# Hybrid decoder step in float32: tokens brought in already turned, and once more by rows

## What is computed

```python
h = rms_norm(x, norm1)                       # mean of squares over 2048 columns
z = h @ w_in                                 # 2048 -> 5120: u (1024), q, f, i, g (1024 each)
pool_out = pool_mix(u, ...)                  # trailing windows 2/4/8/16, per-group 256x256 matrix, pool_scale
o = hgrn2_recurrence(silu(q), 1 - forget, i, log(forget), S0)   # 8 heads, 128x128 state
o = rms(o) * hg_norm * silu(g)
x = x + concat([pool_out, o]) @ w_o          # 2048 -> 2048
h2 = rms_norm(x, norm2)
x = x + (silu(h2 @ w_gate) * (h2 @ w_up)) @ w_down   # 5632 wide
y = rms_norm(x, norm_f)                      # and the new pool and recurrence states
```

## Time and profile before

| what | value |
|---|---|
| median of 3 runs | 1410.99 us (1410.99 to 1411.94) |
| the profiled execution | 1411.39 us |
| its span | 1409.6 us |
| PE matmul busy | 1392.2 us (99%) |
| DVE, ACT, POOL busy | 775.2 us (55%), 579.4 us (41%), 206.9 us (15%) |
| HBM read | 206.43 MB |
| queue of SP | 203.16 MB, 52.6% of 16 engines' span |
| TensorE clock | granted 0.997 of full over the span |

### The profile page before, as it was taken

How to read it: one execution, slowest core, us unless ns; L and a number is a source line. 1 busy time by engine, 2 the same in 40 slices (tenths; PEclk the granted TensorE clock), 3 DMA queues, 4 the chain that set the end, 5 groups by cost and what they waited for, 6 DMA issues and landing times.

```text
span 1409.6 us, 27953 instructions
## 1 busy us (share of the span) xinstructions
PE 1392.2 (99%) x10208; PEld 1377.6 (98%) x10208; DVE 775.2 (55%) x1198; ACT 579.4 (41%) x966; POOL 206.9 (15%) x321
## 2 busy tenths in 40 slices
PE   8999999999999999999999999999999999999996
PEld 7999999999999999999999999999999999999996
DVE  6768888888655544444444444444444444444443
ACT  6535656666433333333333333333333333333443
POOL 0365444445222000000000000000000000000131
PEclk9999999999999999999999999999999999999998
DMA  9556555555655555545655545565554565555453
GB/s 270 145 143 183 152 151 166 165 151 151 166 149 149 149 149 149 149 123 146 179 149 149 149 130 144 146 176 149 149 149 129 146 172 148 149 149 139 124 144 116
DMA packets 408636, 214.53 MB, mean 152 GB/s; under 512 B 4286, under 2 KB 406542, under 8 KB 408597
## 3 DMA queue, kind: packets, MB, share of 16 engines
q1 hardware_dynamic: 389863, 203.16, 52.6%
q10 hardware_dynamic: 18742, 10.95, 2.7%
HBM read 206.43 MB, written 7.89 MB: 152 GB/s over the span
## 4 chain that ended last, share of the span: by engine, by line
PE 98%; DMA 1%; DVE 1%; ACT 0%; issue 0%; DVEq 0%; ACTq 0%
PE bank L426 31%; PE bank L427 31%; PE bank L428 31%; DMA w_raw<-in_w_in 1%; PE bank L540 1%; PE bank L656 0%; PE bank L473 0%; PE bank L698 0%; PE bank L631 0%; PE bank L700 0%; PE bank L699 0%; PE bank L585 0%; PE bank L640 0%; PE bank L755 0%; DVE a_lo L1255 0%; PE bank L618 0%
## 5 line engine op out<-in xcount | busy, mean ns | idle before, releaser
L426 PE MATMUL bank<-a_hi,w_hi 128*128 128x320 f32 x2016 | 627.1, 311 | 0.2
L428 PE MATMUL bank<-a_hi,w_lo 128*128 128x320 f32 x2016 | 623.7, 309 | 0.0
L427 PE MATMUL bank<-a_lo,w_hi 128*128 128x320 f32 x2016 | 623.6, 309 | 0.0
L1185 DVE TENSOR_TENSOR w_lo<-w_raw,w_hi 128x1024 fp32r<-128x1024 f32 (+1 forms) x412 | 457.5, 1151 | 137.5 <-ACT w_hi L813 136.3
L813 ACT ACTIVATE w_hi<-w_raw 128x1024 fp32r<-128x1024 f32 (+1 forms) x412 | 383.4, 967 | 161.0 <-PE bank L428 141.4
L426 PEld LDWEIGHTS bank<-a_hi,w_hi 128*128 128x128 f32 x2016 | 378.7, 188 | 2.4 <-issue 1.6
L427 PEld LDWEIGHTS bank<-a_lo,w_hi 128*128 128x128 f32 x2016 | 378.7, 188 | 0.7
L428 PEld LDWEIGHTS bank<-a_hi,w_lo 128*128 128x128 f32 x2016 | 378.6, 188 | 0.0
L426 PE MATMUL bank<-h_hi,w_hi 128*128 128x320 f32 x704 | 219.0, 311 | 0.0
L428 PE MATMUL bank<-h_hi,w_lo 128*128 128x320 f32 x704 | 217.8, 309 | 0.0
L427 PE MATMUL bank<-h_lo,w_hi 128*128 128x320 f32 x704 | 217.7, 309 | 0.0
(11 more groups left out here) (262 smaller groups left out, 1185.9 us busy)
## 6 DMA issues: line engine op xcount, KB each, us to landing
w_raw<-in_w_gate SPq DMA_DIRECT2D x44, 1024.0 KB, 5.6
w_raw<-in_w_up SPq DMA_DIRECT2D x44, 1024.0 KB, 5.6
w_raw<-in_w_down SPq DMA_DIRECT2D x64, 704.0 KB, 4.8
w_raw<-in_w_in SPq DMA_DIRECT2D x38, 1024.0 KB, 5.8
w_raw<-in_w_o SPq DMA_DIRECT2D x16, 1024.0 KB, 6.0
s<-in_state_hgrn ACTq DMA_DIRECT2D x8, 512.0 KB, 4.3
out<-sn ACTq DMA_DIRECT2D x8, 512.0 KB, 5.4
w_raw<-in_w_in SPq DMA_DIRECT2D x3, 512.0 KB, 8.1
```

What stands on the lines that cost most here:

```text
L426: pe.matmul(out, whi[:, par_, cols], r_hi, start=(k == 0), stop=False)
L427: pe.matmul(out, whi[:, par_, cols], r_lo, start=False, stop=False)
L428: last = pe.matmul(out, wlo[:, par_, cols], r_hi, start=False, stop=(k == last_k))
L1185: dve.tensor_tensor(wlo[:, par_, cols], raw[:, par_, cols], whi[:, par_, cols].bitcast(F32), SUB)\
```

## The change

- The host also lays the inputs out in three new arrays: `x_turned` (partition, tile, token), `w_first_two` (the first 256 columns of `w_in`, by partition), and `params` (all parameter vectors turned).
- `load_x` writes `x_turned` straight into `x1`, one transfer for a chunk. The 48 transposes of tokens, the 16 copies to `x1`, the two transposes of parameters and their copies go. ACT and DVE split from `x1`.
- The tokens by rows are still needed for the squares. They are loaded a second time, in two halves of 1024 columns with three transfers each (`load_tokens`): the first half behind the cache, the second behind the weights of unit 3.
- All squares of ACT stand later, behind the splits of unit 2; the spreading of 1/rms goes from k == 6 to k == 12 of unit 3; the last `lo_piece` of unit 3 goes ahead of the sums.
- `keep_busy` runs 5 matmuls in a row instead of 2 and 1.
- The identity is loaded behind the first chunks.

The diff, cut to its core:

```diff
@@ load_x, load_tokens, first_weights
+        def load_x(eng, chunk):
+            k0, k1 = CHUNKS[chunk]
+            eng.dma_start(x1[:, k0:k1, :], x_turned[:, k0:k1, :]).then_inc(x_loaded[chunk], 16)
+
+        def load_tokens(eng, half):
+            cols = slice(half * HD, (half + 1) * HD)
+            for i in range(2):
+                eng.dma_start(xt[:, i, cols], x_prompt[0, i * P:(i + 1) * P, cols]).then_inc(xt_loaded[half][i], 16)
+            eng.dma_start(xt[0:NS, 2, cols], x_sample.rearrange("b t d -> (b t) d")[:, cols])\
+               .then_inc(xt_loaded[half][2], 16)
...
-                          win_v[:, k0:k1, 0:2 * P]).then_inc(w_first[chunk], 16)
+                          w_first_two[:, k0:k1, :]).then_inc(w_first[chunk], 16)
@@ tensor
-            keep_busy(2)
-            pe.wait_ge(ident_loaded, 16)
-            pe.wait_ge(norm1_loaded, 16)
-            pe.transpose(TK[:, 0:KD], prow[0:KD, :], ident[0:KD, 0:KD]).then_inc(par_t, 1)
-            keep_busy(1)
-            pe.wait_ge(fill_done, 3)
-            pe.wait_ge(x_pad, 1)
-            for k in range(2):
-                x_transposes(k)
+            keep_busy(5)
...
-                for ahead in ((2, 3) if k == 0 else (k + AHEAD,)):
-                    if ahead < KD:
-                        x_transposes(ahead)
...
-                if k == 6:
+                if k == 12:
                     rms_first()
@@ scalar
-                act.wait_ge(xt_t, k + 1)
-                bk = (SA, SB, SC, TV)[k % 4]
-                act.activation(a_hi[:, k, :], bk[:, 0:N], ACT.Copy, scale=pcol("norm1", k)).then_inc(ahi_ready, 1)
-                if k in X_ACT:
-                    act.activation(x1[:, k, :], bk[:, 0:N], ACT.Copy).then_inc(xres_act, 1)
+                for chunk in range(5):
+                    if k == CHUNKS[chunk][0]:
+                        act.wait_ge(x_loaded[chunk], 16)
+                act.activation(a_hi[:, k, :], x1[:, k, :], ACT.Copy, scale=pcol("norm1", k)).then_inc(ahi_ready, 1)
@@ vector
+            dve.wait_ge(ident_loaded, 16)
             diagonals(6, rms_diag)
-            lo_piece(3, 1, 1, HALF[1])
```

More of the change, by code:

```diff
@@ L200, in hybrid_kernel @@
         hi_ready, lo_ready, piece_used, unit_read = (sem(n) for n in ("hi_ready", "lo_ready", "piece_used", "unit_read"))
-        ident_loaded, masks_loaded, norm1_loaded, par_loaded, wp_loaded, cache_loaded, s0_loaded = (
-            sem(n) for n in ("ident_loaded", "masks_loaded", "norm1_loaded", "par_loaded", "wp_loaded",
+        ident_loaded, masks_loaded, par_loaded, wp_loaded, cache_loaded, s0_loaded = (
+            sem(n) for n in ("ident_loaded", "masks_loaded", "par_loaded", "wp_loaded",
                              "cache_loaded", "s0_loaded"))
-        x_loaded = [[sem(f"x_loaded{chunk}{i}") for i in range(3)] for chunk in range(5)]
+        x_loaded = [sem(f"x_loaded{chunk}") for chunk in range(5)]
+        xt_loaded = [[sem(f"xt_loaded{half}{i}") for i in range(3)] for half in range(2)]
         w_first = [sem(f"w_first{chunk}") for chunk in range(5)]
[L206 to L209, removed]
+        first_hi, first_lo, w2_loaded, w3_loaded = (
+            sem(n) for n in ("first_hi", "first_lo", "w2_loaded", "w3_loaded"))
+        fill_done, lb_max, lb_exp, lb_ready = (
+            sem(n) for n in ("fill_done", "lb_max", "lb_exp", "lb_ready"))
         dve_link, newton_step = sem("dve_link"), sem("newton_step")
@@ L357, in load @@
                              view[:, bass.ds(k0, nk), bass.ds(col, P)]).then_inc(raw_loaded[par_], 16)
+            for chunk in range(5):
+                first_weights(sp, chunk)
+                if chunk >= 2:
+                    load_x(sp, chunk)
             sp.dma_start(cst[:, C_ID:C_ID + P], consts[:, C_ID:C_ID + P]).then_inc(ident_loaded, 16)
[L362 to L371, removed]
             sp.wait_ge(first_lo, 3)
@@ L827, in square @@
                 rows, at = (P if i < 2 else NS), 2 * i + half
-                for chunk in ((0, 1, 2), (3, 4))[half]:
-                    act.wait_ge(x_loaded[chunk][i], 16)
+                act.wait_ge(xt_loaded[half][i], 16)
                 after(act, ss_ready, squares[0])
@@ L1212, in _ @@
             dve.memset(epst[:, :], EPS).then_inc(fill_done, 1)
[L1213 to L1214 removed]
+            for bk in (SA, SB, SC):
+                dve.memset(bk[:, 2 * P:4 * P], 0.0)
             dve.memset(stat[:, :], 0.5).then_inc(fill_done, 1)
[L1216 to L1218 removed]
+            dve.wait_ge(par_loaded, 16)
             def lower_bound_max():
[L1222 to L1224 removed]
                 lb0 = 3 * KD
@@ L1261, in _ @@
             lo_piece(2, 0, 0, HALF[0])
-            for k in X_DVE[-2:]:
-                residual(k)
             lower_bound_max()
@@ L1266, in _ @@
             lo_piece(3, 1, 0, HALF[0])
+            lo_piece(3, 1, 1, HALF[1])
             dve.wait_ge(ss_ready, 6)
@@ L1652, in _ @@
         def _(pool):
-            pool.memset(xt[NS:P, 2, :], 0.0).then_inc(x_pad, 1)
             pool.wait_ge(ss_ready, 6)
@@ L1772 @@
     arrays["in_consts"] = constant_table(np)
+    tokens = np.concatenate([inputs["x_prompt"].reshape(TP, D), inputs["x_sample"].reshape(NS, D)])
+    arrays["in_x_turned"] = np.ascontiguousarray(tokens.T.reshape(KD, P, N).transpose(1, 0, 2))
+    first_two = inputs["w_in"][0][:, 0:2 * P].reshape(KD, P, 2 * P)
+    arrays["in_w_first_two"] = np.ascontiguousarray(first_two.transpose(1, 0, 2))
+    arrays["in_params"] = np.ascontiguousarray(
+        np.concatenate([inputs[name].reshape(rows, P) for name, rows in PARAMS]).T)
     args = [nc.dram_tensor(n, a.shape, mybir.dt.from_np(a.dtype), kind="ExternalInput").ap() for n, a in arrays.items()]
```

85 lines of the change are left out of this document (19 added, 66 removed).

## The result

| | before | after |
|---|---|---|
| median | 1411.11 us (13 runs, 1410.53 to 1412.03) | 1414.47 us (13 runs, 1413.44 to 1416.23) |
| ratio | | 1.0025, 95% interval 1.0017 to 1.0034 |
| profiled execution, span | 1411.39 us, 1409.6 us | 1415.68 us, 1413.6 us |
| granted clock over the span | 0.997 | 0.994 |

The kernel became slower by 3.4 us, just over the 0.2% that can be told from no change. The prediction had put 0.55 on no difference and 0.33 on slower. The time lies in the range and 0.3 us from the price of rival B, but it is not the forecast: A's own bounds ended at 1413.8 us. All 13 executions after show a granted clock of 0.994 or 0.995.

The account below looks back on a forecast made before the run. PE's chain was taken as the bound, its start nearly transfer-bound: 7.4 us gained early is eaten by waits of 3.7 and 4.9 us. Unit 4 starts 1.0 us later: 1411.4 + 1.0 = 1412.4, put at 1412.3 us; range 1408.5 to 1416.5.

Parts of the forecast that it names:

- rival B: Wait before unit 4: TensorE falls to its lower clock, costing 2 to 3 us, 1414.8 us in all; chance 0.30.
- A: The forecast case: transfers eat the start's gain, full clock stays; 1412.3 us, by itself 1410 to 1413.8; chance 0.47.
- the clock holds: Part of the forecast case: TensorE keeps its full clock through the 4.9 us standstill before unit 4.
- mark: Unit 4's first matmul, 45.09 us before, forecast at 46.1; the program from there on was to stay unchanged.
- Units 0 and 1 from 8.0 us, done at 22.2: Start of PE: 14.2 us of matmuls from 8.0 us if chunks keep up, ending 7.4 us earlier than before.
- The rate of the start, 365 GB/s: First transfers: 4.83 MB of tokens, first weights, parameters and identity at 365 GB/s from 2.6 us, there by 15.8 us.
- rival C: DMA queue runs faster than assumed: unit 4 starts at 41 to 42 us, about 1407.7 us; chance 0.12.
- Unit 3 at 33.1, waiting 3.7 us: PE before unit 3: waits 3.7 us for unit 3's weights, landing at 30.3 us, and starts at 33.1 us.
- Spreading of 1/rms costs some tenths, covered by the next wait: Unit 3, tile 12: late squares ready at 39 us against 38.9 us, at most some tenths, covered by the following wait.
- Unit 4's weights at 43.7, first matmul at 46.1, a standstill of 4.9 us: Before unit 4: weights land at 43.7 us, splits and handovers take 2.4 us, PE idles 4.9 us.
- Edits costed at nothing: Fewer ACT and DVE copies, POOL's memset, later keep_busy and later identity were each taken to cost nothing.
- Rival D: Doubled tokens run at the cache's 178 GB/s, or everything at 281: unit 4 at 52 us, 1417 to 1418; chance 0.11.

Follow-up runs that it names:

- e2_unit4_first: The changed kernel with unit 4's weights issued ahead of the masks and wp: 1410.86 us, 0.9997 of the kernel before.
- e6_both_orders: The changed kernel with unit 4's weights ahead of masks and wp, and samples' tokens in one transfer to 128 partitions (squares over other columns): 1408.93 us.
- e4_samples_128: The changed kernel with the samples' tokens in one transfer to 128 partitions instead of two to 64 (squares over other columns): 1411.90 us.
- e3_half_tokens: The changed kernel without the second half of the doubled tokens, all squares taken from the first half: 1411.09 us, 0.9998 of the kernel before.
- e5_first_rows: The changed kernel with the first two weight columns read from w_in in 1 KB rows again: 1414.95 us, 1.0025 of the kernel before.
- g1_samples_filled: The changed kernel with samples' tokens in one transfer to 128 partitions and matmuls of ones filling PE's waits before units 3 and 4: 1410.80 us.
- f1_squares_turned: The changed kernel without any second token load, squares taken from the turned tokens and summed by 16 PE matmuls: 1406.85 us, 0.9969 of before.

## Why the prediction was right, and where it was not

**The likeliest case missed one step: "the clock holds".** A gave 1412.3 us from a mark at 46.1 us. Its first half came true: the transfers ate the whole gain of units 0 and 1. Its second half did not, and rival B decided, with its mechanism, its place and nearly its price (2 to 3 us said, 2.5 measured, 1414.8 against 1414.47). That the total agrees to 0.3 us is partly luck: the mark came 0.7 us later than A's, and the profiled execution, which shows that mark, is 1.2 us above the median. The range held only because it took in B. B had a chance of 0.30 because of 3 us after the end of the program in which the clock still reads full, against a forecast standstill of 4.9 us. B asked for a standstill that outlasts those 3 us, and that was too strict: a mean of 0.87 over the window from 44 to 46 us is half speed for its last 0.5 us, so the clock fell some 2.5 us after PE went idle at 43.04 us. The row of the end was also one sample of a scattered time. All ten traces end with the same work, and the clock falls between 0.5 us (`e2_unit4_first`) and 3.2 us (before) after the last matmul: 1.7 us in after, 3.0 us in `e6_both_orders`. The Trainium skill, TensorE: Matmul & The Clock Gate, "HAM oscillation — how this bites in real kernels", describes waits for DMA from which each tile comes back cold; the 0.61 and 0.47 us matmuls from 46.81 us on agree, and unit 3 of the same trace, at full pace behind its 2.48 us, does not.

Point by point:

- **Units 0 and 1 from 8.0 us, done at 22.2.** They began at 7.40 us, but the chunks did not keep up: PE waited 1.7 us for ACT's `a_hi`. Chunk 1 came by ACT's queue behind the parameters, and ACT could begin its `a_hi` only at 9.34 us. Unit 2 began at 23.75 us. 5.8 instead of 7.4 us were gained, and none of it reached the end.
- **The rate of the start, 365 GB/s.** It was 411 to 422 from 6 to 14 us, which the prediction left to rival C. That did not help, since the slow stretches behind it were slower: the transfers to 64 partitions cost 3.3 us, not 2.2 (`e4_samples_128`), and the second half of the tokens 5.3 us, not 4.7 (`e3_half_tokens`).
- **Unit 3 at 33.1, waiting 3.7 us.** 33.64 us and 2.48 us; the wait is shorter because unit 2 itself started later.
- **Spreading of 1/rms costs some tenths, covered by the next wait.** 0.68 us on PE, and in this kernel covered. What was overlooked is DVE: its split of unit 4 stands behind this chain. It is hidden as long as the weights are late, and it is the bound as soon as they are not (`e2_unit4_first`, `e3_half_tokens`).
- **Unit 4's weights at 43.7, first matmul at 46.1, a standstill of 4.9 us.** 44.35, 46.81 and 3.77 us. The way from landing to matmul, 2.4 us, was right (2.46).
- **Edits costed at nothing.** Nothing behind unit 5 changed (mark to end of span 1364.1 to 1364.5 us where the clock held); the first weights' layout moves the landing by 0.4 us.
- **Rival D.** The doubled tokens do not run at the cache's rate: after shows 337 GB/s from 28 to 30 us and 368 from 30 to 32, and drops to 170 (24 to 26 us) and 191 (32 to 34 us) only where a transfer of the samples falls. With that in one transfer to 128 partitions, `e4_samples_128` shows 345 and 361 there.

What stays open is when in a wait the clock falls. `e3_half_tokens` lost it in a wait of 2.20 us, while after kept it through 2.48 us, `e4_samples_128`'s profiled execution through 2.93 us and `e5_first_rows` through 3.00 us, to lose it just behind. The length of the last wait alone doesn't decide it. The 0.5 to 3.2 us at the end of the same program say that the moment differs from execution to execution, so a forecast from one such row needs a wide margin; why it differs, no run here shows.

## What to carry to other kernels

A stage that is nearly bound by transfers gains nothing from less compute if the same edit adds bytes ahead of what is late next: count the queue first, then the engine. A standstill of PE of 2 to 4 us can have two prices, its length and the slow matmuls behind it, and filling it with idle matmuls is a cheap test of the second one. Before loading data a second time for a side result, see whether the first copy can give it: sixteen matmuls for 2.4 us replaced 2.6 MB.

## What was not expected of the hardware

- The granted clock fell 2.2 us (`e3_half_tokens`), 2.4 us (after) and 2.8 us (`e5_first_rows`) into a standstill and held through 2.93 us in `e4_samples_128`; behind the last matmul of the same program it fell after 0.5 to 3.2 us. It stayed low from 45.5 to 52.3 us in after and for 3.4 us each time in `e3_half_tokens` and `e5_first_rows`. With such waits the executions of one kernel fall into two groups 1 to 2 us apart (`e3_half_tokens`, `e4_samples_128`), and filled waits brought them together in `g1_samples_filled`.
- One core drew 411 to 422 GB/s over 8 us (6 to 14 us in after, rows of 2 KB and more), where no window before reached more than 364.
- Two transfers of 0.26 MB to 64 partitions cost the queue 3.3 us more than the same bytes in one transfer to 128.
- DVE's reciprocal on 128x320 took 2.15 us (2.14 in another place, in the kernel before), its other operations of that size in `f1_squares_turned` 0.49 us.
